# Spreading the compression weights of a sparse-attention layer over four weight slots in place of two

## The reference

```python
def hybrid_layer(x, ...):
    h = rms_norm(x, pre_g)
    p = split_columns(h @ w_in + b_in)          # stick-breaking, sparse (nsa), forgetting (fox), latent (mla)
    o_sb = stick_breaking_attention(...)
    o_nsa = native_sparse_attention(...)        # compressed + selected + window keys
    ...
    mix = jnp.concatenate([o * jax.nn.silu(gate) for each branch], axis=-1)
    return x + rms_norm(mix @ w_out, post_g)

def compress_blocks(tok, pos_emb, w1, w2):      # once for keys, once for values
    n_cmp = (S - CMP_LEN) // CMP_STRIDE + 1     # 15 blocks of 32 tokens, stride 16
    blocks = tok[:, gather] + pos_emb
    hidden = jax.nn.silu(blocks.reshape(B, n_cmp, CMP_LEN * d) @ w1)   # w1: 4096 x 128
    return hidden @ w2                                                 # w2: 128 x 128
```

## Time and profile before

| | |
|---|---|
| three executions, median (lowest to highest) | 2135.24 us (2130.68 to 2139.22) |
| the profiled execution, its own time | 2135.86 us |
| its span, first to last instruction | 2134.3 us |
| granted TensorE clock, mean over the span | 0.979 |
| PE busy | 2055.2 us (96%) |
| DVE / ACT busy | 1124.9 us (53%) / 933.0 us (44%) |
| moved by DMA | 361.01 MB, mean 169 GB/s |

### The profile page before, as it was taken

How to read it: one execution, slowest core, us unless ns; L and a number is a source line. 1 busy time by engine, 2 the same in 40 slices (tenths; PEclk the granted TensorE clock), 3 DMA queues, 4 the chain that set the end, 5 groups by cost and what they waited for, 6 DMA issues and landing times.

```text
span 2134.3 us, 30253 instructions
## 1 busy us (share of the span) xinstructions
PE 2055.2 (96%) x10386; PEld 1741.0 (82%) x10386; DVE 1124.9 (53%) x1247; ACT 933.0 (44%) x1215; POOL 131.5 (6%) x179
## 2 busy tenths in 40 slices
PE   7999999998989999998999888999999999999998
PEld 5888988886879998887787776888888888888887
DVE  4464454655556453654557764555544455444443
ACT  5354434444445453443544224454444444443342
POOL 3000000002000000000203630000000000000000
PEclk9999999999999999999999788999999999999999
DMA  7574455665675444664654322566666666656663
GB/s 250 147 238 140 124 158 151 185 194 158 184 202 169 140 141 141 183 195 131 185 158 132 105 79 69 179 188 194 188 187 188 190 192 187 187 188 206 202 203 128
DMA packets 208736, 361.01 MB, mean 169 GB/s; under 512 B 22609, under 2 KB 45696, under 8 KB 208096
## 3 DMA queue, kind: packets, MB, share of 16 engines
q1 hardware_dynamic: 202928, 345.36, 52.7%
q0 software_dynamic: 4816, 13.76, 2.5%
q10 hardware_dynamic: 864, 0.26, 0.1%
HBM read 357.22 MB, written 2.10 MB: 168 GB/s over the span
## 4 chain that ended last, share of the span: by engine, by line
PE 91%; issue 2%; ACT 2%; SPq 1%; DMA 1%; DVE 1%; ACTq 0%; DVEq 0%; POOL 0%; POOLq 0%
PE psum L549 24%; PE psum L550 24%; PE psum L551 24%; PE psum L557 3%; PE psum L559 3%; PE psum L560 3%; SPq L504 1%; DMA raw<-in_w_in_dram 1%; PE psum L606 1%; PE psum L1264 1%; PE psum L615 1%; PE psum L1181 1%; PE psum L855 1%; PE psum L629 1%; PE psum L1200 1%
## 5 line engine op out<-in xcount | busy, mean ns | idle before, releaser
L520 DVE TENSOR_TENSOR wl<-raw,wh 128x1024 fp32r<-128x1024 f32 (+2 forms) x672 | 798.9, 1200 | 765.3 <-ACT wh L513 755.8
L513 ACT ACTIVATE wh<-raw 128x1024 fp32r<-128x1024 f32 (+2 forms) x672 | 691.5, 1037 | 900.1 <-PE psum L551 738.2
L549 PE MATMUL psum<-wh,xh 128*128 128x512 f32 (+2 forms) x1600 | 625.8, 391 | 15.6 <-DVE xl L810 8.0
L550 PE MATMUL psum<-wl,xh 128*128 128x512 f32 (+2 forms) x1600 | 618.5, 387 | 0.0
L551 PE MATMUL psum<-wh,xl 128*128 128x512 f32 (+2 forms) x1600 | 618.2, 386 | 0.0
L549 PEld LDWEIGHTS psum<-wh,xh 128*128 128x128 f32 x1600 | 303.6, 190 | 78.7 <-DVE wl L520 14.9
L551 PEld LDWEIGHTS psum<-wh,xl 128*128 128x128 f32 x1600 | 303.1, 189 | 60.0
L550 PEld LDWEIGHTS psum<-wl,xh 128*128 128x128 f32 x1600 | 303.7, 190 | 57.8
L549 PE MATMUL psum<-wh,mh 128*128 128x512 f32 x384 | 151.2, 394 | 0.0
L551 PE MATMUL psum<-wh,ml 128*128 128x512 f32 x384 | 149.9, 390 | 0.0
L550 PE MATMUL psum<-wl,mh 128*128 128x512 f32 x384 | 149.9, 390 | 0.0
(11 more groups left out here) (342 smaller groups left out, 1646.8 us busy)
## 6 DMA issues: line engine op xcount, KB each, us to landing
raw<-in_w_in_dram SPq DMA_DIRECT2D x264, 512.0 KB, 4.4
raw<-in_w_out_dram SPq DMA_DIRECT2D x96, 512.0 KB, 4.1
raw<-in_w_gate_dram SPq DMA_DIRECT2D x88, 512.0 KB, 3.7
raw<-in_w_up_dram SPq DMA_DIRECT2D x88, 512.0 KB, 3.6
raw<-in_w_down_dram SPq DMA_DIRECT2D x80, 512.0 KB, 4.2
bias<-in_b_in_dram POOLq DMA_DIRECT2D x18, 256.0 KB, 4.2
raw<-in_w_in_dram SPq DMA_DIRECT2D x16, 268.0 KB, 2.9
raw<-in_nsa_cmp_w_k_dram SPq DMA_DIRECT2D x32, 128.0 KB, 2.3
```

Source lines behind the costliest of these rows:

```text
L513: act.activation(wh[:, n % SPLIT_SLOTS, 0:k, 0:unit.n], raw[:, n % RAW_SLOTS, 0:k, 0:unit.n], ACT.Copy).then_inc(hi_done, 1)
L520: dve.tensor_tensor(out=wl[:, n % SPLIT_SLOTS, 0:k, 0:unit.n], in0=raw[:, n % RAW_SLOTS, 0:k, 0:unit.n], in1=wh[:, n % SPLIT_SLOTS, 0:k, 0 ...
L549: pe.matmul(o, ah_[:, kt, tok], hi_w, start=first, stop=False)
L550: pe.matmul(o, ah_[:, kt, tok], lo_w, start=False, stop=False)
```

## The change

The eight c units go to slots 6, 7, 8 and 9, two in each, as the third and sixth of six units: slots 6 and 7 are now w w c w w c, slots 8 and 9 f f c f f c. Since the last c is now multiplied in slot 9, every step of the compressed branch comes two slots later: the hidden layer goes from stage 8 to 10, `w2` from 9 to 11, the turned keys from 10 to 12, the scores from 11 to 13, and the two turns of the probabilities from 12 and 13 to 15 and 16 (stage 14 uses all of the PSUM space they need). The mids on ACT and DVE follow. No work is added or taken away.

```diff
--- before.py
+++ after.py
@@ -123,8 +123,9 @@
 
     units = [Unit("cmp_w1", tuple((c, HD) for c in range(0, 4 * HD, HD)), (2 * j, 2 * j + 1), "cmp", None, "cmp",
                   CMP_STRIDE, j == 0, j == CMP_STRIDE // 2 - 1) for j in range(CMP_STRIDE // 2)]
-    for first, slot in zip((0, SLOT_UNITS), CMP_SLOTS):
-        slots[slot] = [u for pair in zip(slots[slot], units[first:first + SLOT_UNITS]) for u in pair]
+    for i, slot in enumerate(CMP_SLOTS):
+        a, b, c, d = slots[slot]
+        slots[slot] = [a, b, units[2 * i], c, d, units[2 * i + 1]]
     return slots
 
 
@@ -149,7 +150,7 @@
     return slots + slots_of(rest[2:])
 
 
-CMP_SLOTS = (6, 7)
+CMP_SLOTS = (6, 7, 8, 9)
 CMP_ROWS = 2 * 16 + 4
 LAYER_SLOTS = with_compress_units(slots_of(input_units("w_in", GROUPS))) + output_slots()
 WIN_SLOTS = NG * 2
@@ -1205,12 +1206,12 @@
                     return second()
                 stages = {
                     2: mla_turn_latents, 3: mla_queries_and_keys, 4: mla_values_and_ropes,
-                    8: lambda: both(mla_turn_ropes, nsa_compress_hidden), 9: lambda: both(nsa_turn, nsa_compress_out),
-                    10: lambda: both(mla_scores, nsa_turn_compressed_keys),
-                    11: lambda: both(lambda: pe_transpose_probs(prob), compressed_scores),
-                    12: lambda: both(sb_scores, lambda: turn_compressed(0)),
-                    13: lambda: both(sb_decays, lambda: turn_compressed(1)),
-                    14: sb_and_mla_values, 15: lambda: nsa_scores(4), 16: lambda: pe_transpose_probs(prob),
+                    8: mla_turn_ropes, 9: nsa_turn, 10: lambda: both(mla_scores, nsa_compress_hidden),
+                    11: lambda: both(lambda: pe_transpose_probs(prob), nsa_compress_out),
+                    12: lambda: both(sb_scores, nsa_turn_compressed_keys),
+                    13: lambda: both(sb_decays, compressed_scores),
+                    14: sb_and_mla_values, 15: lambda: both(lambda: nsa_scores(4), lambda: turn_compressed(0)),
+                    16: lambda: both(lambda: pe_transpose_probs(prob), lambda: turn_compressed(1)),
                     17: lambda: nsa_scores(5), 18: lambda: pe_transpose_probs(prob), 19: nsa_values,
                     21: fox_all_scores, 22: lambda: pe_transpose_probs(prob),
                     23: lambda: pe_values([(probT, lambda kb, h: fox_v[:, kb, h * HD:(h + 1) * HD])], bank_pair(0)),
@@ -1462,7 +1463,6 @@
                     act.drain()
                     act.activation(prob[:, :], prob[:, :], ACT.Ln, bias=1.0)
                     act.drain().then_inc(s("sb_softplus"), 1)
-                    compressed_turned(0)
 
                 def biased_features(name, dst, b0):
                     act.wait_ge(s(name + "_scaled"), place.once)
@@ -1487,16 +1487,16 @@
                     3: lambda: scaled(qnT[:, :, :].rearrange("p h t -> p (h t)"), st[:, 0:1024], MLA_SCALE),
                     4: lambda: (compressed_high(),
                                 scaled(v_mla[:, :, :].rearrange("p b n -> p (b n)"), st[:, 0:1024], 1.0)),
-                    7: lambda: (scaled(cmp_sum[0:2 * CMP_ROWS, :], psum[0:2 * CMP_ROWS, 7, :], 1.0), small_nonlinear()),
-                    8: lambda: (hidden_silu(),
-                                scaled(qrT[0:64, 0:4, :].rearrange("p h t -> p (h t)"), st[0:64, 0:1024], MLA_SCALE)),
-                    9: lambda: scaled(qkT[:, 0:4, :].rearrange("p h t -> p (h t)"), st[:, 0:1024], SCALE),
-                    10: lambda: act_softmax(place, "mla", prob),
-                    11: lambda: (compressed_exp(), act_copy_half(probT), biased_features("sb_k", sb_kT, 4)),
+                    7: small_nonlinear,
+                    8: lambda: (scaled(qrT[0:64, 0:4, :].rearrange("p h t -> p (h t)"), st[0:64, 0:1024], MLA_SCALE)),
+                    9: lambda: (scaled(cmp_sum[0:2 * CMP_ROWS, :], psum[0:2 * CMP_ROWS, 7, :], 1.0),
+                                scaled(qkT[:, 0:4, :].rearrange("p h t -> p (h t)"), st[:, 0:1024], SCALE)),
+                    10: lambda: (hidden_silu(), act_softmax(place, "mla", prob)),
+                    11: lambda: (act_copy_half(probT), biased_features("sb_k", sb_kT, 4)),
                     12: sb_softplus,
-                    13: lambda: (act.activation(prob[:, :], st[:, 0:1536], ACT.Exp), compressed_turned(1)),
-                    15: lambda: act_softmax(place, "sel", prob),
-                    16: lambda: act_copy_half(pT_sel),
+                    13: lambda: (act.activation(prob[:, :], st[:, 0:1536], ACT.Exp), compressed_exp()),
+                    15: lambda: (act_softmax(place, "sel", prob), compressed_turned(0)),
+                    16: lambda: (act_copy_half(pT_sel), compressed_turned(1)),
                     17: lambda: (act_softmax(place, "win", prob), biased_features("fox_k", fox_kT, 12)),
                     18: lambda: act_copy_half(pT_win),
                     21: lambda: (act_softmax(place, "fox", prob), act_gate("nsa")),
@@ -1777,10 +1777,8 @@
                 def nsa_turned():
                     dve.tensor_copy(flat(qkT[:, 4:6, :]), st[:, 1024:1536])
                     scaled_features(0, sb_qT, 0)
-                    compressed_keys()
 
                 def mla_softmax():
-                    dve.tensor_copy(kcT[:, :], st[:, 1536:1536 + NCMP])
                     dve_softmax(place, "mla")
 
                 def compressed_softmax():
@@ -1790,7 +1788,6 @@
                     dve.drain()
                     tt(p, z, bc(cmp_max, NCMP), ALU.subtract)
                     dve.drain().then_inc(s("cmp_shifted"), 1)
-                    dve_copy_half(probT)
                     dve.wait_ge(s("cmp_exp"), place.once)
                     dve.tensor_reduce(out=cmp_den, in_=p, axis=AX, op=ALU.add)
                     dve.drain()
@@ -1854,8 +1851,9 @@
                     2: positions_and_row_factors,
                     3: keys_and_compressed_tokens, 4: compressed_blocks, 5: nsa_queries,
                     7: small_group, 8: nsa_ropes, 9: nsa_turned, 10: mla_softmax,
-                    11: lambda: (features(1, sb_kT).then_inc(s("sb_k_scaled"), 1), compressed_softmax()), 12: sb_softplus,
-                    13: lambda: biased(6, [(0, 512, sb_v[:, :, :])]),
+                    11: lambda: (features(1, sb_kT).then_inc(s("sb_k_scaled"), 1), dve_copy_half(probT), compressed_keys()),
+                    12: lambda: (dve.tensor_copy(kcT[:, :], st[:, 1536:1536 + NCMP]), sb_softplus()),
+                    13: lambda: (compressed_softmax(), biased(6, [(0, 512, sb_v[:, :, :])])),
                     14: lambda: (dve.tensor_copy(flat(o_mix["sb"][:, :, :]), st[:, 0:1024]),
                                  dve_scaled_out(o_mix["mla"], st[:, 1024:2048])),
                     15: lambda: (dve_softmax(place, "sel"), gate_probs(1), scaled_features(1, fox_qT, 8)),
```

## The result

Six executions of the changed kernel gave a median of 2146.95 us (2144.17 to 2153.01), six of the kernel before beside them 2135.26 us: a ratio of 1.0060, interval [1.0038, 1.0081]. The change makes the kernel slower by 0.6%. The forecast was 2130.0 us, its range 2124.5 to 2137.0; the time lies outside, near the last rival's 2144.5. The profiled execution took 2144.17 us (span 2142.6, before 2134.3), at a mean granted clock of 0.975 (before 0.979). It is the fastest of the six: the traces show 8.3 us of the 11.7 that lie between the medians, and what follows explains those 8.3.

The account below looks back on a forecast made before the run. SP's issue queue was taken as the limit (4.09 us a pair against PE's 2.77). Per layer 6.9 us go and 4.5 come, 4.8 won in both, plus 1.4 of clock: 2135.86 becomes 2129.7, said as 2130; range 2124.5 to 2137.

Parts of the forecast that it names:

- the last rival: Slots 8 and 9: mids 7 and 8 start 3.3 us later behind late loads, 2144.5 us; chance 0.08.
- Part 1: Loads of slots 6 and 7: the 6.9 us loss per layer shrinks to 1.5 us ahead of the first f.
- the zero gap: Ahead of the first f: by the skill's 50 ns dispatch SP is never behind, 1.5 us less per layer.
- Part 2: Mids 7 and 8 behind six splits: new PE waits of 1.6 us before stage 8, 1.4 before stage 9.
- rows 5: Profile rows of the same pieces: 1.86 us until the last is issued, 2.5 us landing; basis for the 1.6 us wait.
- The upper bound of 4.7 us: Ahead of stage 9: the longest wait, if the sixth unit's load lands after 6.2 us instead of 2.5.
- the slower rival: Sixth units' loads in slots 8 and 9 land late, 11.2 us lost a layer, 2144.5 us; chance 0.08.
- Part 3: Moved stages and mids, slots 10 to 16: PE's work is the same sum, no new gap, no cost.
- The clock: Slot 8, layer one: the clock's fall goes, 1.4 us won; possibly zero, or 1.4 lost.

Follow-up runs that it names:

- e4: The kernel before, with each c unit loaded by two DMAs in place of four: 2129.16 us, ratio 0.9978.
- e1: The changed kernel with the 1 MB load of `post_g` moved behind mid 11: 2135.10 us, ratio 1.0004.
- e5: Control: the kernel before, with the `post_g` load moved behind mid 11: 2133.59 us, ratio 0.9992.
- e3: The changed kernel with the c units back in slots 6 and 7, only the stages and mids two slots later: 2138.84 us, ratio 1.0020.

## Why the prediction was wrong

**Part 1 was about right.** A gap of 1.5 us a layer was forecast, 2.1 and 2.3 are left; the most that could be won, 6.9, was read rightly. Its reason was only in part right. I put all of it on the number of SP's issues. e4 takes away two of a pair's seven, and the loss falls by 2.0 and 2.9 of 6.9 us. The rest is transfers or the queue behind SP, and is not told apart here. On the Trainium skill's dispatch figure of about 50 ns for GpSimd's path ("DMA: Bandwidth & Descriptors", anatomy of one DMA): an issue takes SP 0.37 us at the shortest here, and a gap of 2.1 us is left, so the zero gap did not come true.

**Part 2 failed, at the load of slot 9's sixth unit.** The step reads "I take 1.6, since rows 5 are the same pieces", and the same for stage 9 with 1.4. Mid 7 and mid 8 themselves ran as long as foreseen (6.48 and 6.25 us). Their start was wrong. The prediction let the sixth split start when PE has used the slot's second unit; in the trace the load comes later than that and sets the start:

- Stage 9, layer one: the last split ahead of mid 8 ends 11.66 us after slot 9's first matmul (152.75 - 141.09), not 8.32. The fifth unit's load took 7.2 us (141.64 to 148.88) and the sixth's 5.6 (144.87 to 150.43), not 2.5. The upper bound of 4.7 us, with 6.2 us landing, was the true case; that the wait is 3.49 and not 4.6 is only because slot 9 itself took 1.1 us longer at the lower clock. e1 shows the cause: with `post_g` out of the way the c loads land in 3 us and the wait is 1.08 us, and 1.50 in layer two.
- Stage 8, layer one: the last split ends 9.76 us after the first f, 1.4 us later than forecast. SP's last piece of that unit was out at 4.6 us and not at 3.1, since the splits were still late from the gap ahead of the first f; the prediction took them as caught up. It landed at 7.4 us (130.44), where PE had used the second unit at about 6. Hence 2.65 us and not 1.6.

The argument against the slower rival, that the DMA share in slot 8 leaves room, looked at the wrong stretch: the load that collides is issued at mid 7's end, so in slot 9. The kernel before has it in its trace at 143.64 us, and the earlier trace rows with their 6.2 us landing were its footprint, for in e5, without it, the same loads take 4.6. I had these rows, took them as a bound and gave the case 0.08. That the time is near this rival's 2144.5 is partly luck: it has waits of 5.0 and 4.7 us and no new fall of the clock, and measured were 2.2 to 3.5 us and a clock that cost 3.9.

**Part 3 failed too: "what moves without a price" has one.** e3 puts the moved stages at 0.2% [0.07%, 0.33%], some 4 us, where I had none. Its profiled execution shows 1 us of it as gaps behind stage 8, which has 1.7 us less work now and hides less of slot 9's first split, and 1.5 us as slot 11's clock. The rest of that is not located.

**The clock was counted with the wrong sign.** Slot 8 won its 1.4 us as forecast. But slots 9, 10 and 11 of layer one and slot 9 of layer two lost about 1.1, 1.3, 1.5 and 1.4 us (slot 9 against 13.42 us, slots 10 and 11 against before). Slots 9 and 10 stand behind the new waits, and that these bring the fall is argued and not shown: in e1 slot 9 of layer one fell as far behind 2.02 us, and slot 8 of layer two behind 1.40. Slot 11's fall goes with the moved stages (e3). The forecast gave gaps of 1.5 us the benefit of the doubt and had no term for gaps of 3, nor for the clock behind stage 10.

**The sum, with the measured terms.** Won a layer: 6.9 - 2.1 = 4.8, and 6.9 - 2.3 = 4.6. Paid: 2.65 + 3.49 = 6.1, and 2.19 + 0.41 + 3.39 = 6.0. Net waits 1.3 + 1.4 = 2.7 us lost where 4.8 were to be won. The clock adds 1.1 + 1.3 + 1.5 + 1.4 - 1.4 = 3.9. That is 6.6 of the 8.3 us. Another 1.0 is in stage 8: from its first turn to slot 9's first matmul it is 1.80 us and, less the wait of 0.41, 1.37 us, where the same ten turns took 1.09. Then 0.7 are left, about 0.3 a layer behind slot 11.

Still open: what the loss ahead of the first f consists of besides issues; what in stage 10 lowers slot 11's clock; where the rest of e3's 4 us lies; and why slot 10 keeps clock 1.00 in layer two behind a wait of 3.39 us, and has 0.87 in layer one behind one of 3.49.

## What to carry to other kernels

Work that is spread to relieve one place takes the slack of the places it goes to, and a long elementwise step behind more splits starts as late as the last load in front of it: read the landing time in the stretch where the load will stand, with every transfer that another engine starts there, and not where the piece stands now. A lookahead that is refilled by the same engine that does the long step runs dry while that step lasts, and all that waited for its end is issued at once. Where the limit is many small transfers, try first to make them fewer (e4, ratio 0.9978) before moving them (ratio 1.0060, and 1.0004 without the collision). Steps that move along with the work are not free because their sum is the same: measure them alone, as e3 does (1.0020).

## What the runs showed of the hardware

- The same 128 KB pieces landed in 2.9 to 3.1 us (e1) and in 5.6 to 5.8 us beside a 1 MB broadcast load on GpSimd's queue, which itself took 7.2 us. The 512 KB loads of 135 to 160 us landed in 6.2 us beside it (kernel before) and in 4.6 without it (e5).
- Three issues of w took SP 1.49 us in the kernel before, and 1.49 to 2.60 in e4: the time of an issue is not fixed. What it depends on is not shown.
- The granted clock was low behind waits of 2.65 and 3.49 us in layer one and 2.19 in layer two (0.87 to 0.92 in the slots after), in e1 also behind 2.02 and 1.40 us (0.93 and 0.89), and not in layer two's slot 10 behind 3.39 us (1.00). In slot 11 it was 0.87 with no wait ahead (the changed kernel, e1, e3).
